# Cached keys and mLSTM states: turned copies in DRAM, loaded straight into the products' operands

## The reference: one step of a hybrid streaming encoder

```python
def _band_attention_sample(q, k, v, k_cache, v_cache, rel_bias):
    k_all = jnp.concatenate([k_cache, k.astype(k_cache.dtype)], axis=1)
    v_all = jnp.concatenate([v_cache, v.astype(v_cache.dtype)], axis=1)
    s = jnp.einsum('bqhd,bkhd->bhqk', q, k_all).astype(jnp.float32) * (Dh ** -0.5)
    s = s + _rel_bias(rel_bias, T, W + T, W)[None]
    p = jax.nn.softmax(s, axis=-1).astype(v_all.dtype)
    o = jnp.einsum('bhqk,bkhd->bqhd', p, v_all).reshape(B, T, H * Dh)
    return o, k_all[:, T:], v_all[:, T:]

# in _mlstm_chunk, with the carried C (v-index, k-index) and n:
    num = w_inter[..., None] * jnp.einsum('bhvk,bhtk->bhtv', C, q) + jnp.einsum('bhts,bhsv->bhtv', w_intra, v)
    den = w_inter * jnp.einsum('bhk,bhtk->bht', n, q) + jnp.sum(w_intra, axis=-1)
    C_new = decay[..., None, None] * C + jnp.einsum('bhs,bhsv,bhsk->bhvk', ws, v, k)
```

## Time and profile before

| what | value |
|---|---|
| median of 3 runs | 2232.58 us (2232.32 to 2236.16) |
| span of the profiled execution | 2230.6 us, 34685 instructions |
| PE busy | 2210.9 us, 99% of the span |
| DVE, ACT, POOL busy | 837.7, 490.9, 413.3 us |
| mean share of the 16 DMA engines, bytes | 304.36 MB, mean 136 GB/s |
| granted clock of PE | 0.999 of full speed |

### The profile page before, as it was taken

The page is one execution under the profiler, slowest core; times in us unless marked ns, Lnnn a source line. Parts: engine busy times, 40 slices in busy tenths (PEclk is TensorE's granted clock), DMA queues, the critical chain, the costliest instruction groups (busy, mean ns, idle before and its releaser), DMA issues.

```text
span 2230.6 us, 34685 instructions
## 1 busy us (share of the span) xinstructions
PE 2210.9 (99%) x14090; PEld 2058.1 (92%) x14090; DVE 837.7 (38%) x1446; ACT 490.9 (22%) x835; POOL 413.3 (19%) x249
## 2 busy tenths in 40 slices
PE   8999999999999999999999999999999999999998
PEld 6999999999999999999999999999998998888887
DVE  7940131313222111138657332332421463353634
ACT  6510222222221111110111111111101023333432
POOL 0122221212222122223122222212221210000000
PEclk9999999999999999999999999999999999999999
DMA  9422314142242433342322224443334556564552
GB/s 372 133 80 99 142 62 166 54 156 90 77 151 81 165 110 125 139 129 87 102 90 78 73 74 144 132 134 113 109 108 169 205 195 240 170 246 159 200 205 94
DMA packets 166862, 304.36 MB, mean 136 GB/s; under 512 B 28508, under 2 KB 105948, under 8 KB 164208
## 3 DMA queue, kind: packets, MB, share of 16 engines
q1 hardware_dynamic: 158704, 286.77, 37.8%
q10 hardware_dynamic: 8064, 16.25, 2.2%
HBM read 244.88 MB, written 76.92 MB: 144 GB/s over the span
## 4 chain that ended last, share of the span: by engine, by line
PE 94%; DVE 3%; DMA 2%; ACT 0%; SPq 0%; issue 0%; POOLq 0%; DVEq 0%; ACTq 0%
PE G L950 21%; PE G L952 21%; PE G L951 21%; PE G L1333 3%; PE X L1333 3%; PE G L1334 3%; PE X L1335 3%; PE X L1334 3%; PE G L1335 3%; PE X L1088 1%; PE X L1310 1%; PE X L1048 1%; PE X L1079 1%; DMA cv<-u_scratch 1%; DVE cv L475 1%; PE X L1202 1%
## 5 line engine op out<-in xcount | busy, mean ns | idle before, releaser
L950 PE MATMUL G<-hhi,whi 128*128 128x384 f32 x2832 | 963.9, 340 | 0.0
L952 PE MATMUL G<-hhi,wlo 128*128 128x384 f32 x2832 | 948.4, 335 | 0.0
L951 PE MATMUL G<-hlo,whi 128*128 128x384 f32 x2832 | 948.0, 335 | 0.0
L950 PEld LDWEIGHTS G<-hhi,whi 128*128 128x128 f32 x2832 | 532.2, 188 | 21.1 <-issue 13.4
L951 PEld LDWEIGHTS G<-hlo,whi 128*128 128x128 f32 x2832 | 532.4, 188 | 0.8
L952 PEld LDWEIGHTS G<-hhi,wlo 128*128 128x128 f32 x2832 | 532.0, 188 | 0.0
L924 POOL CAST whi<-wr 128x1024 fp32r<-128x1024 f32 x115 | 124.4, 1082 | 1383.8 <-PE G L952 1168.1
L926 POOL TENSOR_TENSOR wlo<-wr,whi 128x1024 fp32r<-128x1024 f32 x115 | 283.8, 2468 | 9.2
L1350 ACT ACTIVATE ev<-G 128x384 f32<-128x384 f32 x162 | 79.3, 489 | 720.9 <-PE G L952 720.8
L2182 DVE TENSOR_TENSOR olo<-orw,ohi 128x1024 fp32r<-128x1024 f32 x96 | 112.1, 1219 | 155.1 <-ACT ohi L1604 154.6
L1604 ACT ACTIVATE ohi<-orw 128x1024 fp32r<-128x1024 f32 x96 | 95.3, 1050 | 165.6 <-PE X L1335 61.5
(11 more groups left out here) (392 smaller groups left out, 1994.4 us busy)
## 6 DMA issues: line engine op xcount, KB each, us to landing
wr<-w_in_t SPq DMA_DIRECT2D x118, 512.0 KB, 5.4
orw<-w_out_t SPq DMA_DIRECT2D x96, 512.0 KB, 5.3
u_scratch<-ev SPq DMA_DIRECT2D x174, 192.0 KB, 1.9
x_lo<-x_t SPq DMA_DIRECT2D x7, 1536.0 KB, 12.5
xin<-x_all SPq DMA_DIRECT2D x9, 1024.0 KB, 12.9
yr<-y_scratch SPq DMA_DIRECT2D x12, 768.0 KB, 7.7
xo<-x_all SPq DMA_DIRECT2D x3, 3072.0 KB, 11.7
kc<-k_cache SPq DMA_DIRECT2D x8, 1024.0 KB, 5.5
```

The lines of the kernel that those rows point to most:

```text
L950: mm(G[:, j, 0:GC], whi[:, kh, k], hhi[:, kk, hs], start=(kk == 0), stop=False)
L951: mm(G[:, j, 0:GC], whi[:, kh, k], hlo[:, kk, hs], start=False, stop=False)
L952: return mm(G[:, j, 0:GC], wlo[:, kh, k], hhi[:, kk, hs], start=False, stop=(kk == 15))
```

## The change

The host passes two more arrays. `k_cache_t` holds each stream's keys as (128, 4, 512): partition, head pair, key, which is what `sKT` held in its first 512 columns. `c_init_t` holds each head's states with the k-index on the partitions, 8 streams x 128, which is what `ct8` held in its first 128 columns. The untransposed arrays stay: `k_cache` for the shifted cache that is an output, `c_init` for `cnat`.

In the streams PE has no key transposes, ACT and DVE no evictions of them, and the semaphores `kt_mm` and `kt_ev` are gone. `kT` has two buffers, in the places of `kc` and `sKT`; the 16 new keys get a small tile `skn` of their own. The wait for the loaded keys (`kc_in`) moves behind block 1. SP loads the keys of stream b + 1 into the other buffer, and waits before that for the scores of stream b - 1 (`ss_mm`, which now starts at 1, so DVE's wait on it counts one more).

In the heads PE has no transposes of `cnat`, ACT no evictions. `ct8` has two buffers, each filled by a DMA of its own; PE waits for `ct_in` and `n_in_ct` ahead of the product. DVE's scaling of `cnat` waits for its load (`c_in`) itself.

```diff
-        kc = sb(st3, "kc", [128, 4, 512])
+        kT = [sb(st3, "kT0", [128, 4, 512])]
         vc = sb(st3, "vc", [128, 4, 512])
-        sKT = sb(st3, "sKT", [128, 4, SK])
+        kT.append(sb(st3, "kT1", [128, 4, 512]))
+        skn = sb(st3, "skn", [128, 4, DT])
...
-        ct8 = sb(st5f, "ct8", [128, NSTR, 129])
+        ct8 = [sb(st5f, "ct80", [128, NSTR, 129])]
...
+        sb(st5f, "place_of_CT", [128, 1404])
+        ct8.append(sb(st5f, "ct81", [128, NSTR, 129]))
...
-            def load_keys(b):
+            def load_keys(b, s):
                 sp.wait_ge(s_mm, 33)
-                sp.wait_ge(kt_mm, 4 * b + 4)
-                sp.dma_start(kc[:, :, :], k_cache[b].rearrange("(t p) n -> p t n", p=128)).then_inc(kc_in, 16)
+                sp.wait_ge(ss_mm, b)
+                sp.dma_start(kT[s][:, :, :], k_cache_t[b]).then_inc(kc_in, 16)
...
             sp.dma_start(cnat[:, 0], c_init[0]).then_inc(c_in[0], 16)
+            sp.dma_start(ct8[0][:, :, 0:128], c_init_t[0]).then_inc(ct_in[0], 16)
             sp.dma_start(cnat[:, 1], c_init[1]).then_inc(c_in[1], 16)
+            sp.dma_start(ct8[1][:, :, 0:128], c_init_t[1]).then_inc(ct_in[1], 16)
...
                 if h < 2:
+                    sp.wait_ge(tp_done, h + 1)
+                    sp.dma_start(ct8[h][:, :, 0:128], c_init_t[h + 2]).then_inc(ct_in[h], 16)
                     sp.wait_ge(c_out[h], 16)
...
-                    pe.wait_ge(kc_in, 16 * b + 16)
                     pe.wait_ge(sy_done, b + 1)
-                    for t in range(4):
-                        for hp in range(4):
-                            last = tr(X[:, t, 128 * hp:128 * hp + 128], kc[:, t, 128 * hp:128 * hp + 128], ident[:, :])
-                        last.then_inc(kt_mm, 1)
...
-                    pe.wait_ge(kt_ev, 4 * b + 4)
+                    pe.wait_ge(kc_in, 16 * b + 16)
                     pe.wait_ge(kq_done, 4 * b + 4)
                     for hp in range(4):
-                        mm(X2[32 * hp:32 * hp + 32, 0:512], qblk[:, hp], sKT[:, hp, 0:512], start=True, stop=True)
+                        mm(X2[32 * hp:32 * hp + 32, 0:512], qblk[:, hp], kT[s][:, hp, :], start=True, stop=True)
...
-                pe.wait_ge(c_in[h % 2], 16 * (h // 2) + 16)
                 if h:
                     pe.wait_ge(cu_done, h)
-                for hf in range(2):
-                    for b in range(4):
-                        last = tr(X[:, hf, 128 * b:128 * b + 128], cnat[:, h % 2, 4 * hf + b], ident[:, :])
-                    last.then_inc(ctt_mm, 1)
                 pieces(HEAD_AT + 3 * h, HEAD_AT + 3 * h + 1)
-                pe.wait_ge(ctt_ev, 3 * h + 3)
+                pe.wait_ge(ct_in[h % 2], 16 * (h // 2) + 16)
+                pe.wait_ge(n_in_ct, h + 1)
...
-                    for t in (0, 2):
-                        act.wait_ge(kt_mm, 4 * b + t + 5)
-                        fn(sKT[:, :, 128 * t:128 * t + 128], X[:, t].rearrange("p (h n) -> p h n", h=4),
-                           ACT.Copy).then_inc(kt_ev, 1)
...
-                for hf in range(2):
-                    act.wait_ge(ctt_mm, 2 * h + hf + 1)
-                    fn(ct8[:, 4 * hf:4 * hf + 4, 0:128], X[:, hf].rearrange("p (b n) -> p b n", b=4),
-                       ACT.Copy).then_inc(ctt_ev, 1)
...
-                    for t in (1, 3):
-                        dve.wait_ge(kt_mm, 4 * b + t + 5)
-                        cp(sKT[:, :, 128 * t:128 * t + 128], X[:, t].rearrange("p (h n) -> p h n", h=4)).then_inc(kt_ev, 1)
-                    cp(sKT[:, :, 512:SK], sk[:, :, bs]).then_inc(kq_done, 1)
+                    cp(skn[:, :, :], sk[:, :, bs]).then_inc(kq_done, 1)
...
-                dve.wait_ge(ctt_mm, 2 * h + 2)
+                dve.wait_ge(c_in[s], 16 * (h // 2) + 16)
```

More of the change, by code:

```diff
@@ L34, in encoder_program @@
 def encoder_program(nc, x_all, x_t, w_in_t, w_gate, w_out_t, g_in, g_out, bias_p, bias_s, b_if, m_init,
-                    k_cache, v_cache, c_init, n_init, conv_w, conv_buf, s5_par, s5_b, s5_c, s5_s0,
+                    k_cache, k_cache_t, v_cache, c_init, c_init_t, n_init, conv_w, conv_buf, s5_par, s5_b, s5_c, s5_s0,
                     s5_d, w_glu, b_glu,
@@ L349, in encoder_program @@
         tq_in, c_in = sem("tq_in"), [sem("c_in0"), sem("c_in1")]
-        ctt_mm, ctt_ev = sem("ctt_mm"), sem("ctt_ev")
+        ct_in, n_in_ct = [sem("ct_in0"), sem("ct_in1")], sem("n_in_ct")
         qm_done, wkm_done = sem("qm_done"), sem("wkm_done")
@@ L618, in attention @@
                     if g == 6 and last:
-                        load_keys(0)
+                        load_keys(0, 0)
                 sp.wait_ge(y_done, 8 * i + 9)
@@ L647, in streams @@
                     if not (last and s == 1):
-                        load_keys(b + 1)
+                        load_keys(b + 1, 1 - s)
                     sp.dma_start(kv_new[i, s], uT[5 + 4 * i + s, :, 512:NT]).then_inc(kv_out, 16)
@@ L884, in _ @@
                          (u_stored[0], 16), (u_stored[1], 16), (u_stored[2], 16), (s_mm, 1), (s_add, 1),
-                         (tp_mm, 1), (tp_evac, 1), (y_done, 1), (ay_stored, 16), (kt_mm, 4), (so_mm, 3), (sy_done, 1),
+                         (tp_mm, 1), (tp_evac, 1), (y_done, 1), (ay_stored, 16), (ss_mm, 1), (so_mm, 3), (sy_done, 1),
                          (g5_stored, 16), (ct_done, 1), (hn_done, 1), (my_done, 2), (my_stored, 16),
@@ L1119, in _ @@
                         gemm(24 + 2 * i + t, kh, j)
-                    pe.wait_ge(kt_ev, 4 * b + 4)
+                    pe.wait_ge(kc_in, 16 * b + 16)
                     pe.wait_ge(kq_done, 4 * b + 4)
                     for hp in range(4):
-                        mm(X2[32 * hp:32 * hp + 32, 0:512], qblk[:, hp], sKT[:, hp, 0:512], start=True, stop=True)
+                        mm(X2[32 * hp:32 * hp + 32, 0:512], qblk[:, hp], kT[s][:, hp, :], start=True, stop=True)
                     for hp in range(4):
-                        last = mm(X2[32 * hp:32 * hp + 32, 512:SK], qblk[:, hp], sKT[:, hp, 512:SK], start=True, stop=True)
+                        last = mm(X2[32 * hp:32 * hp + 32, 512:SK], qblk[:, hp], skn[:, hp], start=True, stop=True)
                     last.then_inc(ss_mm, 1)
@@ L1283, in _ @@
                     pair = slice(32 * (b // 2), 32 * (b // 2) + 32)
-                    mm(o[pair], qm[:, 128 * b + 32 * (b // 2):128 * b + 32 * (b // 2) + 32], ct8[:, b], start=(b % 2 == 0), stop=False)
+                    mm(o[pair], qm[:, 128 * b + 32 * (b // 2):128 * b + 32 * (b // 2) + 32], ct8[h % 2][:, b], start=(b % 2 == 0), stop=False)
                 mm(o, WT[:, h], vn1[:, h], start=False, stop=True).then_inc(tp_done, 1)
@@ L1905, in _ @@
                     cp(qblk[64:128, :, DT:2 * DT], sq[64:128, :, bs]).then_inc(kq_done, 1)
-                    dve.wait_ge(ss_mm, b + 1)
+                    dve.wait_ge(ss_mm, b + 2)
                     stt(sS[:, :], X2[:, 0:SK], 0.125, sbias[:, :], MUL, ADD).then_inc(ss_add, 1)
@@ L2116, in spread_head @@
                     dve.wait_ge(tp_done, h)
-                cp(ct8[:, :, 128], nin[:, h]).then_inc(ctt_ev, 1)
+                cp(ct8[h % 2][:, :, 128], nin[:, h]).then_inc(n_in_ct, 1)
                 cp(qm[:, :].rearrange("p (b n) -> p b n", b=NSTR)[:, :, 0:DT],
@@ L2312 @@
         "b_if": a["mlstm_b_if"][0].reshape(2, 4).T, "m_init": a["state_mlstm_m"][0].T,
-        "k_cache": a["cache_attn_k"][0].reshape(NSTR, 512, 512), "v_cache": a["cache_attn_v"][0].reshape(NSTR, 512, 512),
-        "c_init": a["state_mlstm_C"][0].transpose(1, 2, 0, 3), "n_init": a["state_mlstm_n"][0].transpose(2, 1, 0),
+        "k_cache": a["cache_attn_k"][0].reshape(NSTR, 512, 512),
+        "k_cache_t": a["cache_attn_k"][0].reshape(NSTR, 512, 4, 128).transpose(0, 3, 2, 1), "v_cache": a["cache_attn_v"][0].reshape(NSTR, 512, 512),
+        "c_init": a["state_mlstm_C"][0].transpose(1, 2, 0, 3), "c_init_t": a["state_mlstm_C"][0].transpose(1, 3, 0, 2), "n_init": a["state_mlstm_n"][0].transpose(2, 1, 0),
         "conv_w": a["conv_w"][0].reshape(3, 4, 128).transpose(2, 0, 1),
```

4 lines of the change are left out of this document (removed).

## The result

The changed kernel takes 2219.55 us (median of 4 runs, 2217.8 to 2221.7) against 2232.45 for the kernel before (2232.3 to 2236.2) beside it: a ratio of 0.9942, 95% interval 0.9930 to 0.9954. So it is 13 us faster, where I forecast 17 (2215.6), and the time lies half a microsecond above my range. The profiled execution is the slowest of its four, 2221.71 us, with a span of 2219.6.

What follows compares the result with a forecast made beforehand. The prediction took PE (TensorE) to bound the kernel, busy 2210.9 of 2230.6 us. Keys 14.0 plus states 3.9 less a new wait 0.9 gave 17.0 us gained, so 2215.6 us, range 2213.8 to 2219.0.

Steps and rivals of the forecast that it cites:

- Keys, 14.0 us: In the streams, 16 key transposes leave PE's queue in each of 8 streams at 1.75 us: 14.0 us gained.
- The rule that I had weighed: For PE's transposes, about 81 ns each, not 109: 160 give 13.0 us, time 4 us higher; left out of the sum.
- States, 3.9 us: In four heads, PE's state transposes and a seam go, 0.97 us each: 3.9 us gained.
- The wait in stream 0, -0.9 us: Ahead of stream 0's first score product, PE newly waits for `qblk`: 0.92 us lost, bounds 0.4 and 1.4.
- At worst ... cost nothing: In the streams, weights queued behind the keys land a microsecond late at worst; some 8 us of cover remain, cost nothing.
- the sum itself: Whole kernel: 14.0 + 3.9 - 0.9 = 17.0 us gained, profiled 2213.6, median of runs 2215.6.
- (c): The new wait in stream 0 lets PE's clock fall to half pace once: 2.7 us lost, 2218.3; 4%.
- (b): At the heads, the first state load lands late by up to 3 us: 2215.6 to 2218.6; 8%.
- (d): In the streams, weights land late and PE waits at each tile's start: slower, 2239.6 at 3 us each; 3%.
- (e): Something unseen takes up freed slots, place not named: half the gain, 2224.1, 3%; all of it, 2232.6, 1%.

Runs made afterwards that it cites:

- third set moved: Third set of output weights issued ahead of the last conv stores and `xo`, in the kernel before: 2240.89 us; the same in the changed kernel: 2228.97 us.
- the two kernels with both moves: Third set of output weights issued ahead of conv stores and `xo`, DVE's wait for `go` put later: changed kernel 2216.13 us, kernel before 2231.34 us.
- the two kernels with moved code: 128 more instructions at the start of PE's program: changed kernel 2235.81 us, kernel before 2255.95 us.
- the kernel before again: The kernel before, unaltered, timed and profiled a second time: 2234.42 us.
- the changed kernel again: The changed kernel, unaltered, timed and profiled a second time: 2221.11 us, ratio 0.9942.
- the states alone: Only the states' half of the change made to the kernel before, keys still turned on PE: 2232.32 us, ratio 0.9992.
- keys alone: Only the keys' half of the change made to the kernel before, states still turned on PE: 2224.78 us, ratio 0.9959.

## Why the prediction was right, and where it failed

**Keys, 14.0 us: right.** Each stream is 1.74 us shorter, no seam was gained (28.96 us from stream 1 to 2, forecast 28.95). The rule that I had weighed, some 81 ns for a weight load and matmul of 128 columns (the Trainium skill, "TensorE: Matmul & The Clock Gate", "Back-to-back issue gap"), would have given a time 4 us higher than the forecast, 2219.6, which is nearly what was measured. That is chance: the 16 transposes gave back 1.74 us, 109 ns each, as the rows said, and the 4 us went elsewhere.

**States, 3.9 us: slightly too much.** The four heads gave 15.23 - 11.68 = 3.55 us, 0.89 each, where I had 0.97. I took the difference of two stretches of 72 matmuls at different places, 13.54 and 12.57 us; the stretch that replaced the first takes 12.67 (from 1591.35 to 1604.02).

**The wait in stream 0, -0.9 us: right in cause, too small.** It was 1.32 us by the row and 1.40 by the starts (rows show 1.0 to 1.7 in six other profiles with the turned keys, above 1.4, the end that I gave, in three of them). The copies ended at 746.41 and not 746.08 since `sbias` landed later, and PE came 0.24 us earlier. My bound was half a microsecond on either side of one landing time, and a landing varies by more.

**"At worst ... cost nothing", for the weights behind the keys: right in the streams, and their end was left out.** In streams 1 to 7 there is no wait. Behind the last stream SyncE waits for four small stores of `sz`, the fourth of which landed 2.87 us after its issue in place of 1.63, a fetch of code lying at the same moment; all that follows is late by as much, POOL starts its cast late, and PE waits 0.28 us for `wlo`. A second wait, 0.35 us ahead of S5, has no releaser in the profile; the kernel before shows one of 0.25 there with its third set moved. By the starts of the matmuls PE falls back 0.55 us at each of the two places, and that is the 1.1 us that this stretch lost. The sum had no term for it.

```profile
990.29 1.04 POOL L929 CAST whi<-wr 128x1024 fp32r<-128x1024 f32 x1 [17.27 <-DMA wr<-w_in_t]
```

```profile
994.71 0.44 PE L955 MATMUL G<-hhi,whi 128*128 128x384 f32 x1 [0.28 <-POOL wlo L931]
```

**The step that failed is the sum itself.** "14.0 + 3.9 - 0.9" carries the gain through everything behind the heads unchanged and so puts the last product at nothing, where it lost 5.2 us in the profile and 2.3 by the medians; my only look at the last product was at its first matmul. There I should have read the two blocks behind it: `olo` of the third set was ready 0.1 us before PE wanted it. PE's wait of 0.73 us for `ylo` gave the loads, which are issued when PE ends the last G block, that much of a lead; with the wait gone in the changed kernel, they are issued 0.9 us later against PE (0.19 us after the product's start in place of -0.70), and everything from there is late. But the kernel before had no such lead in its second profile either (`yr` issued at 0.11), and there it waited 1.50 us: the margin of 0.1 us was that of one execution. Two terms give that wait, by an estimate: the lead, 0.8 us, and `xo`'s 512 packets, 24 ns longer each and 32 to each of 16 DMA engines, 0.8 us. With terms as measured the sum comes out: 14.0 + 3.6 - 1.5 for stream 0 (1.77 us lost there against 0.27) - 0.8 at the end of the streams (both between the two kernels with both moves) = 15.3 us, and 15.2 is what the medians give between these two. So of the 4 us that I missed, on the medians, 2.3 are the last product's, 0.8 the end of the streams, 0.6 the wait in stream 0 and 0.3 the states.

**Rivals.** (c), half a pace after a wait, happened, but elsewhere: behind 1851.28 the starts of matmuls of 512 columns go from 0.23 to 0.43 us, and the block takes 1.7 us more, at 0.91 of the clock; I had priced it at 2.7 for 17 matmuls behind a much longer idle time. Behind the new wait in stream 0 the G products start 0.17 apart, full pace. The Trainium skill's section "Part 1: The HAM clock gate" on the same page says that idling costs the clock. The trace agrees behind waits of 1.78 us (changed kernel), 2.18, 2.24, 3.29 and longer, and in the attention of the two kernels with moved code even behind 1.41 and 1.65; it shows no fall behind 1.50 (the kernel before again), 2.22 (the changed kernel again) and 2.95 (the kernel before, code moved). (b) and (d) didn't happen: no wait ahead of the products with `ct8`, none in streams 1 to 7. (e), something unseen that takes up freed slots, is what did happen, with a quarter of the gain and not half.

**What stays open.** Why the changed kernel loses 3.9 to 5.6 us in the last product and the kernel before 0.4 to 1.9. A fall of the clock, where there is one, is 1.7 us of it. Part of it is the lead of 0.7 us. But the states alone kept most of that lead (`yr` issued at -0.61) and still lost 4.2. The times of landing after the product's start suggest the fetch of code as the other part (from the traces; "fourth" and "eighth" are the last loads of the second and third set):

| kernel | fetch of PE's code | fourth | eighth |
|---|---|---|---|
| before | -15.2, 12.2 | 10.9 | 30.5 |
| before, again | -14.5, 12.3 | 11.9 | 32.0 |
| after, code moved | -14.1, 12.9 | 12.1 | 32.6 |
| states alone | -7.1, 19.7 | 11.1 | 32.7 |
| keys alone | -6.5, 20.4 | 12.0 | 33.7 |
| before, code moved | 6.2, 26.3 | 13.6 | 33.4 |
| after | 6.6, 28.4 | 15.7 | 34.1 |
| after, again | 6.1, 28.1 | 15.2 | 34.0 |

A fetch that falls among the loads goes with a later fourth load, 13.6 to 15.7 against 10.9 to 12.1, one that falls at 12 to 13, behind these loads, with the earliest third set (though 32.6 is hardly less than the 32.7 of the states alone). The kernels with other orders of loads agree on the fourth load: 13.1 and 13.3 with a fetch at 5.3, and 10.9, 11.6 and 12.0 with one at 10.0, 10.7 and 0.8. It was not shown by an edit that moves the fetch and nothing else: the one that I made changed the loop as well. The added tensors in DRAM aren't needed for an explanation: `xo`'s packets took 385 ns each in the first profile of the kernel before and 402 to 433 in all others, those of the kernel before among them (410, 413, 420).

## What to carry to other kernels

When time is taken out of the bounding engine, look at each later place where its work meets transfers that start on its own signal, and read how long the data were ready before they were wanted; a margin near zero there eats the gain, though no wait shows yet. Put loads that are wanted soon ahead of large ones that are wanted late in the same queue, and look for waits on the late ones in the consumer's program as well: here moving the loads alone cost 7 to 8 us, and together with the wait it gave 3 to 5 by the medians (the wait alone was not tried). A kernel with a shorter program fetches its code at other moments, so a small difference far from an edit need not come from what the edit does: here the same change gave 13 us as it stood, 15 with both moves and 20 with the code moved, by the medians.

## What the runs showed of the hardware

- Loads of one queue waited for what was issued ahead of them: 512 KB of `orw` took 3.5 to 6.4 us with nothing but their like in the queue (in the first 45 us of the last product), and 16.0 to 19.2 when issued within 14 us behind 3 MB of `xo`. The Trainium skill, "DMA: Bandwidth & Descriptors", "Queues, rings and completion order", says that each DMA engine takes a ring's descriptors in order, and that a later one may finish first. The trace agrees with both: in the three profiles with a fetch at 6 us the store issued behind the fourth load landed 0.1 to 0.4 us before it.
- PE's code came in 69 or 70 packets of 16 KB during the execution, 0.9 to 2.3 us each. A loop of the program that ran without fetches (342 to 611 us in the kernel before) had them all along once 128 instructions stood ahead of it, and PE lost 7 us. A store of 64 KB landed in 1.6 us, and in 2.4 to 2.9 with such a packet at its issue.
- A pair of semaphore waits that were already met, one instruction, took 88 ns on PE.
- PE's clock fell to its lower level behind waits of 1.4 and 1.8 us in two profiles and not behind 2.2 and 2.95 in others; each fall in the last product cost 1.5 to 2.5 us in the block behind it.
